# A two-layer streaming-encoder trunk in fp32 pairs: a new order of the attention steps, half of the convolution's taps moved and read from PSUM, and inverse roots by logarithm and exponential

## What is computed

```python
def swiglu(x, w_gate, w_up, w_down):          # 1024 -> 2816 -> 1024
    return (silu(x @ w_gate) * (x @ w_up)) @ w_down

def even_mixer(h, ...):                        # h = rmsnorm(x)
    u, g, q, k, v, f_logit = split(h @ w_in)   # 512 columns each, f_logit 8
    a = u * sigmoid(g)
    a = causal_depthwise_conv(a, conv_w) + conv_b      # 31 taps
    a = silu(rmsnorm(a, conv_norm))            # norm over 512 channels
    q, k = rmsnorm(q, q_norm), rmsnorm(k, k_norm)      # per head, 64 wide
    o = forgetting_attention(q, k, v, log_sigmoid(f_logit + b_f))
    return concatenate([a, o]) @ w_out
# forgetting_attention: logits = q k^T / 8 + cum_f[q] - cum_f[k], causal, softmax, @ v; 8 heads
```

## Time and profile before

| | |
|---|---|
| median of three runs | 1962.81 us |
| profiled execution | 1965.04 us, its span 1963.2 us |
| TensorE matmul busy | 1889.5 us (96%), 8333 instructions |
| VectorE busy | 915.5 us (47%) |
| ScalarE busy | 621.6 us (32%) |
| GpSimd busy | 330.2 us (17%) |
| mean DMA | 89 GB/s |

### The profile page before, as it was taken

The page is one execution under the profiler, slowest core; times in us unless marked ns, Lnnn a source line. Parts: engine busy times, 40 slices in busy tenths (PEclk is TensorE's granted clock), DMA queues, the critical chain, the costliest instruction groups (busy, mean ns, idle before and its releaser), DMA issues.

```text
span 1963.2 us, 22410 instructions
## 1 busy us (share of the span) xinstructions
PE 1889.5 (96%) x8333; PEld 1540.9 (78%) x8333; DVE 915.5 (47%) x1016; ACT 621.6 (32%) x803; POOL 330.2 (17%) x276
## 2 busy tenths in 40 slices
PE   7999999998876899999999999999999999999999
PEld 5888888875555688888888888888888888888887
DVE  6443433379875564343334443433365454343321
ACT  4333332225433443333223333332222333333221
POOL 3111101115444211111101111110113021111000
PEclk9999999999877899999999999999999999999999
DMA  5333333221100143333332333343233333333431
GB/s 142 99 98 96 102 111 100 75 79 54 32 1 6 56 121 96 96 96 108 103 99 75 96 96 96 96 118 99 72 97 96 97 97 96 96 96 100 118 105 42
DMA packets 341356, 174.86 MB, mean 89 GB/s; under 512 B 6256, under 2 KB 340284, under 8 KB 341308
## 3 DMA queue, kind: packets, MB, share of 16 engines
q1 hardware_dynamic: 337052, 172.12, 30.3%
q10 hardware_dynamic: 4256, 2.11, 0.4%
HBM read 172.10 MB, written 2.10 MB: 89 GB/s over the span
## 4 chain that ended last, share of the span: by engine, by line
PE 88%; DVE 7%; ACT 2%; issue 2%; POOL 1%; DMA 0%; SPq 0%; ACTq 0%; POOLq 0%; DVEq 0%
PE bank L1188 29%; PE bank L1189 29%; PE bank L1190 29%; DVE conv L901 3%; DVE w_lo L871 1%; DVE pt_lo L1094 1%; ACT w_hi L587 0%; DMA x_rows<-in_x 0%; DVE h_rough L1032 0%; PE bank L1417 0%; POOL probs_a L547 0%; POOL conv L559 0%; PE bank L1244 0%; DVE neg_max L1087 0%; ACT probs_a L737 0%
## 5 line engine op out<-in xcount | busy, mean ns | idle before, releaser
L871 DVE TENSOR_TENSOR w_lo<-raw,w_hi 128x1024 fp32r<-128x1024 f32 (+2 forms) x308 | 403.0, 1309 | 718.6 <-ACT w_hi L587 718.2
L1188 PE MATMUL bank<-xg_hi,w_hi 128*128 128x512 f32 x1728 | 678.3, 393 | 8.1 <-DVE w_lo L871 4.8
L1189 PE MATMUL bank<-xg_lo,w_hi 128*128 128x512 f32 x1728 | 674.0, 390 | 0.0
L1190 PE MATMUL bank<-xg_hi,w_lo 128*128 128x512 f32 x1728 | 673.8, 390 | 0.0
L587 ACT ACTIVATE w_hi<-raw 128x1024 fp32r<-128x1024 f32 (+2 forms) x308 | 340.3, 1105 | 793.0 <-PE bank L1190 792.9
L1188 PEld LDWEIGHTS bank<-xg_hi,w_hi 128*128 128x128 f32 x1728 | 325.4, 188 | 86.3 <-issue 10.8
L1189 PEld LDWEIGHTS bank<-xg_lo,w_hi 128*128 128x128 f32 x1728 | 325.5, 188 | 68.1 <-issue 1.2
L1190 PEld LDWEIGHTS bank<-xg_hi,w_lo 128*128 128x128 f32 x1728 | 325.3, 188 | 67.8
L1188 PE MATMUL bank<-h_hi,w_hi 128*128 128x512 f32 x704 | 274.5, 390 | 0.0
L1190 PE MATMUL bank<-h_hi,w_lo 128*128 128x512 f32 x704 | 274.0, 389 | 0.0
L1189 PE MATMUL bank<-h_lo,w_hi 128*128 128x512 f32 x704 | 273.9, 389 | 0.0
(11 more groups left out here) (184 smaller groups left out, 1171.3 us busy)
## 6 DMA issues: line engine op xcount, KB each, us to landing
raw<-in_ffn_w_gate SPq DMA_DIRECT2D x88, 512.0 KB, 3.8
raw<-in_ffn_w_up SPq DMA_DIRECT2D x88, 512.0 KB, 3.8
raw<-in_ffn_w_down SPq DMA_DIRECT2D x64, 704.0 KB, 4.5
raw<-in_od_w_in SPq DMA_DIRECT2D x24, 512.0 KB, 3.7
raw<-in_ev_w_in SPq DMA_DIRECT2D x20, 512.0 KB, 3.8
raw<-in_ev_w_out SPq DMA_DIRECT2D x16, 256.0 KB, 2.7
raw<-in_od_w_out SPq DMA_DIRECT2D x8, 512.0 KB, 3.7
x_rows<-in_x SPq DMA_DIRECT2D x4, 512.0 KB, 7.4
```

The source lines that it names most:

```text
L871: dve.tensor_tensor(w_lo[:, u % 2, 0:n], raw[:, u % 4, 0:n], raws(w_hi[:, u % 2, 0:n]), ALU.subtract)\
L1188: pe.matmul(dst, a[0], b[0], start=start, stop=False)
L1189: pe.matmul(dst, a[0], b[1], start=False, stop=False)
L1190: return pe.matmul(dst, a[1], b[0], start=False, stop=stop)
```

## The change

1. Taps. VectorE keeps two tiles (0 and 2), ScalarE with GpSimd gets two (1 and 3). VectorE's source tile now lies in PSUM bank 7: tile 0 is written there directly, tile 2 is copied there by ScalarE when tile 0 is done. Only the last 10 VectorE taps, one a step in attention, read it from SBUF. The forget logits move to bank 5. VectorE's taps are put behind every unit of A_GATE (at most 4), and ScalarE's start in A_GATE (13), then 29 in qk, 12 in v, and 2 in each of the first four steps of attention.
2. Head norms. `head_sum` runs two units late instead of one, with four buffers for squares. The fans of the last three tiles move into attention's steps 0 to 2. The split of v starts tile by tile (`v_done`).
3. Attention. On each engine the work of a step has a new order: the inverse of the last step's sums first, then the maxima, the output's split, the transposed probabilities' split (one step later than before), and the taps. ScalarE does the split ahead of the exponentials. `weigh` is one step later. 22 steps in all. GpSimd scales the probabilities one step later in its program.
4. Convolution's norm. The sum over partitions moves from step 14 to 16, behind the last scores; its silu and split move into the first units of the out phase.
5. Out phase. The attention half comes first for all eight output tiles, and the first three quarters of its first two units are issued in steps 18 and 19.
6. Inverse roots. ScalarE computes Ln and then Exp with factor -0.5; the reciprocals of the norms are gone, the Newton step stays.

```diff
-    DVE_TILES, ACT_TILES = list(range(CB - 1)), [CB - 1]
-    TAPS_A, TAPS_QK = [7, 7, 8, 8], [2, 4, 4, 3, 4, 0, 4, 4]
-    TAPS_T = 3
-    ACT_TAPS_QK, ACT_TAPS_V = [0, 3, 4, 4, 4, 4, 4, 4], 4
+    DVE_TILES, ACT_TILES = [0, 2], [1, 3]
+    TAPS_A, TAPS_QK = [0, 4, 3, 4, 4, 4, 4, 4], [2, 2, 4, 2, 4, 1, 4, 4]
+    TAPS_T = 1
+    ACT_TAPS_A, ACT_TAPS_QK, ACT_TAPS_V, ACT_TAPS_T = [3, 3, 4, 3], [2, 3, 4, 4, 4, 4, 4, 4], [4, 4, 4], 2
-    V_FANS = [(1, 1), (1, 3), (2, 1), (2, 3), (3, 0), (3, 2)]
+    V_FANS = [(1, 2), (2, 1), (3, 1)]
-    TURN_LAG = 2
-    PV_LAG = 3
-    OUT_LAG = PV_LAG + 1
-    STEPS = PAIRS + OUT_LAG
-    NEXT_SPLIT = (12, 16)
+    INV_AT, TURN_AT, PT_AT, PV_AT, OUT_AT = 1, 2, 3, 5, 8
+    STEPS = TB * (AB - 1) + OUT_AT + 2
+    NEXT_SPLIT = (12, 14)
+    A_SQ, A_SUM = [4, 6, 8, 14], PAIRS
+    MERGE_AT = (STEPS - 4, STEPS - 3)
+    SILU_AT = [(0, 2), (0, 3), (1, 0), (1, 1)]
...
             def norm_root(ready, n, mean, out_log, out_rough, done):
+                logs[0] += 1
                 act.wait_ge(ready, n)
-                act.activation(out_root, mean, ACT.Sqrt).then_inc(done, 1)
+                act.activation(out_log, mean, ACT.Ln).then_inc(log_ready, 1)
+                act.wait_ge(log_ready, logs[0])
+                act.activation(out_rough, out_log, ACT.Exp, scale=-0.5).then_inc(done, 1)
...
+                        if i == 1:
+                            act.wait_ge(conv_done, 1)
+                            act.activation(bank[7][:, :], a_in[:, DVE_TILES[1], :], ACT.Copy).then_inc(conv_moved, 1)
...
                 elif ph.kind == "v":
...
                     qk_high(0)
                     split_hi(ph, 0, 2)
+                    conv_taps(ACT_TAPS_V[0])
                     qk_high(1)
+                    conv_taps(ACT_TAPS_V[1])
                     qk_high(2)
+                    split_hi(ph, 0, 3)
+                    conv_taps(ACT_TAPS_V[2])
                     qk_high(3)
-                    split_hi(ph, 0, 3)
-                    conv_taps(ACT_TAPS_V)
-                    for n in range(AB, QK - 1):
-                        qk_high(n)
+                    qk_high(4)
...
             def conv_taps(n, late=False):
+                    src = a_in[:, b, :] if late else bank[7][:, :]
-                        op = dve.scalar_tensor_tensor(conv[:, b, shift:S], a_in[:, b, 0:S - shift], wk,
+                        op = dve.scalar_tensor_tensor(conv[:, b, shift:S], src[:, 0:S - shift], wk,
                                                       conv[:, b, shift:S], ALU.mult, ALU.add)
...
+                            split_lo(ph, g, 3)
                             dve.wait_ge(root_ready, ph.norm + 1)
-                            link(dve.reciprocal(rough[:, :], root[:, :]))
-                            split_lo(ph, g, 3)
                             invert(mean_sq[:, :], rough[:, :], corr[:, :], rstd[:, :]).then_inc(rstd_ready, 1)
...
                 for t in range(STEPS):
+                    if 0 <= t - INV_AT < PAIRS:
+                        cols = slice(2 * (t - INV_AT), 2 * (t - INV_AT) + 2)
+                        dve.wait_ge(exp_done, 2 * (t - INV_AT) + 2)
+                        dve.reciprocal(row_inv[:, cols], row_sum[:, cols]).then_inc(inv_ready, 1)
                     if t < PAIRS:
                         for i in (2 * t, 2 * t + 1):
...
-                    if 0 <= t - TURN_LAG < PAIRS:
...
+                    if 0 <= t - PT_AT < PAIRS:
...
-                    if t < PAIRS:
-                        dve.wait_ge(exp_done, 2 * t + 2)
-                        dve.reciprocal(row_inv[:, 2 * t:2 * t + 2], row_sum[:, 2 * t:2 * t + 2]).then_inc(inv_ready, 1)
...
+                    if QK - 3 + t < QK:
+                        qk_low(QK - 3 + t)
-                    conv_taps(TAPS_T)
+                    conv_taps(TAPS_T, late=True)
...
                 for t in range(STEPS):
                     if t < PAIRS:
                         scores(t)
+                    if t == A_SUM:
+                        pe.wait_ge(exp_done, 2 * t)
+                        pe.wait_ge(a_added, CB - 1)
+                        pe.matmul(bank[3][:, :], ones[:, :], sq_sum[:, :], start=True, stop=True).then_inc(a_sum, 1)
+                    if QK - 3 + t < QK:
+                        fan(QK - 3 + t)
+                    for par in range(2):
+                        chunk = every(t, PV_AT + par, 2, CHUNKS)
+                        if chunk is not None:
+                            weigh(chunk, par)
+                    if 0 <= t - TURN_AT < PAIRS:
+                        turn(t - TURN_AT)
+                    if t in MERGE_AT:
+                        n = MERGE_AT.index(t)
+                        pe.wait_ge(wlo_ready, A_OUT.unit0 + n + 1)
+                        merge_part(A_OUT, 0, n, list(range(CB - 1)))
...
-                        if i:
-                            head_sum(i - 1)
+                        if i >= 2:
+                            head_sum(i - 2)
```

306 lines of the change are left out of this document (160 added, 146 removed).

## The result

The changed kernel takes 1919.3 us, the median of 4 runs (1918.7 to 1921.0); the kernel before takes 1964.1 in the same series (1962.7 to 1965.5). The ratio is 0.9773, with a 95% interval of 0.9756 to 0.9790: 44.8 us less, against 45 forecast. The sum is right, but most of its terms are not, and they are what the rest is about.

The account below looks back on a forecast made before the run. Outside the first mixer TensorE was the bound; gains lay between 382 and 700 us, in waits behind VectorE's queue. Gains 12 + 9 + 20 + 4 = 45 us from 1962.8 gave 1918 us, range 1903 to 1945.

Parts of the forecast that it names:

- the first scores: Start of attention: as a sign of being right, the first scores come some 21 us earlier.
- A_GATE and qk, 12 forecast: First mixer stages: 114 us become 102, with PSUM taps at 0.70 us and 2.6 us of waits.
- The two-input rule: VectorE taps: only two SBUF inputs contend with GpSimd reading SBUF; by it A_GATE and qk gain 1 us more.
- v, 9 forecast: v stage: 48 us become 38.5 to 39, TensorE waiting 7 us for the last unit's w_lo.
- ScalarE waiting for GpSimd's adds in qk or v: qk and v: a sign that the forecast is wrong, ScalarE waiting for GpSimd's conv adds.
- that rival: qk and v: GpSimd becomes the bound, adds at 1.9 us, gain 30, 1933 us; chance 0.09.
- Attention, 20 forecast: First to last scores: 91.2 us fall by 20; four steps at 5.0, eleven at 4.6, the 11.1 us wait gone.
- The loop that I found last: Attention step: scores, maxima, output split, both splits of the step before, then the second tile's turn; 4.3 us.
- The steps don't get shorter: Attention: handshakes and low clock set the pace, only the stall goes, gain 10 there, 1928 us; chance 0.17.
- Tail, 4 forecast: Last scores to next phase: 65.0 us become 60.5 to 61, with waits listed for splits, Ln and Exp, weights and clock.
- The other norms, 0 forecast: Six norms of other phases: Ln, load and Exp end 0.9 us ahead of w_hi, so they gain and cost nothing.
- The rule by which the load between them would fall away: Ln and Exp share one table set, needing one load; by it tail and v would each be 1.3 us shorter.

Follow-up runs that it names:

- tile2_sbuf: Changed kernel with VectorE's second conv tile of taps read from SBUF instead of its PSUM copy: 1931.1 us.
- v_quiet: Changed kernel with v's weight splits ahead of ScalarE's taps, four taps moved into attention, the logits' splits and scan moved: 1911.6 us.
- sum_at_14: Changed kernel with the convolution norm's sum over partitions put back in front of step 14's scores: 1930.4 us.
- old_split: Changed kernel with the splits inside an attention step back in their old order, weigh steps as changed: 1927.0 us.
- merge_late: Changed kernel without the early start of the output projection, all its products behind the attention: 1918.5 us.
- before_no_late_taps: Kernel before the change with 36 of its 38 VectorE taps in attention left out (convolution incomplete): 1939.2 us.
- more_taps: Changed kernel with two extra VectorE taps from SBUF in each of 16 attention steps, results thrown away: 1931.1 us.
- both: Changed kernel with old_split's order and v_quiet's v part, its eight ScalarE taps placed four and four: 1911.9 us.
- both_pv4: The kernel both with the weigh steps one step earlier, as in the kernel before: 1909.9 us.
- v_split_first: Changed kernel with w_lo of v's last unit ahead of k's low part and the logits' splits, k's high part before ScalarE's third four taps: 1916.9 us.

## Why the prediction was right, and where it was not

The sum, 45 us less, was met (44.8 by the medians, 46.0 by the profiled executions) because errors cancel: v was 8.6 and A_GATE with qk 2.6 too high, the attention 6.2 and the tail 3.9 too low, and 2.1 came from a start that varies by itself. So close a sum is luck; what held is that all of the gain lies in the mixer and most of it in the attention. Of the signs that I had named, the first scores came 12 us earlier and not 21, mainly because v gave nothing.

*A_GATE and qk, 12 forecast, 9.4 measured (10.9 by the four kernels with 103.1).* The price of a tap from PSUM was right: 0.70 taken, 0.733 measured, and tile2_sbuf shows that it is the operand's place and not GpSimd's leisure. The two-input rule of the Trainium skill ("SBUF — State Buffer", "Who interferes with whom") agrees with the taps of tile2_sbuf in one stretch: 0.717 us with one input in PSUM, 1.273 with both in SBUF. But that price is not the whole gain: undoing it for tile 2 took back 3.4 us in this stage (4.9 against the 103.1). The kernel before waited 5.3 us here for the squares of the head sums and the changed one not at all; I hadn't priced that, and no run separates the later head sums from the shorter queue of VectorE. What I left out is that the other instructions of VectorE pay for GpSimd's adds: the scan of the logits stands in front of a `w_lo`, which itself takes 1.98 us, and TensorE waits 2.06 at 463.81. v_quiet, with the scan behind it, has 101.6 us, my 102.

*v, 9 forecast, 0.4 measured.* The mechanism was the right one, TensorE waiting for `w_lo` of v's last unit; the chain was mis-sized. I had 31 us from qk's end to that `w_lo`; it ended at 522.29, 37.9 after 484.40. Newton's instructions are 1.64 and 1.62 us and not 0.7, two of the logits' splits 1.5 and not 0.7, both under GpSimd's adds; and I counted ScalarE's products as lying in between, while four of them (2.9 us) stood in front of `k_hi`. The rest, 9.8 us for 7.5 behind the wait, is a wait of 0.9 for `v_lo` and the slow clock (0.80 from 522.3 to 532.1 us). I had named ScalarE waiting for GpSimd's adds in qk or v as a sign that GpSimd is the bound: it came, in five waits of 2.9 us in all, 0.38 of them in the queue at whose end TensorE waited 11.5. GpSimd wasn't the bound (an add took 1.35 us on average, and that rival needed 1.9); what I hadn't asked is what stands behind the products in ScalarE's queue, and behind `k_lo` in VectorE's.

*Attention, 20 forecast, 26.2 measured.* The loop that I found last is the one that TensorE's nine waits for `pt_lo` show, and by rows it gave 4.3 us; steps 8 to 11 took 4.13. The step of the sum that failed is the 0.3 that I added for the clock: it was 1.00 from step 6 on, 0.93 over the eleven steps. The eleven steps took 47.0 us, 4.27 each for 4.6, and the first four 4.5 for 5.0: 5.6 of the 6.2. In the first four the reason was wrong: I had GpSimd busy for 20 us there, and it was busy for 12.7 of 18.0, while the clock was 0.72 and TensorE waited 2.7 us for the probabilities and 1.8 for `pt_lo`. "The steps don't get shorter" fell with 4.13 us. The moved sum was worth 8 to 11 us (sum_at_14), and the earlier trace rows had 11.1.

*Tail, 4 forecast, 7.9 measured.* I listed 7.5 us of waits and slow clock; 2.7 came, 1.5 for `cat_lo`, 0.8 for `w_lo` and 0.4 for `pt_lo`, at full clock. By old_split, the new order of `cat_hi` and `cat_lo` is what keeps the tail short, which I hadn't seen as a gain at all; the early merges, which I had taken for one, bring nothing (merge_late).

*The other norms, 0 forecast, 0.0 measured.* This is right as described: a load lies between Ln and Exp, and ScalarE's `w_hi` still waits for TensorE. ffn2's norm:

```profile
662.94 0.63 ACT L623 ACTIVATE log_mean<-mean_sq 128x512 f32<-128x512 f32 x1 [0.59 <-DVE mean_sq L974]
663.59 1.28 ACT L625 ACT_TABLE_LOAD   x1
664.88 0.63 ACT L625 ACTIVATE rough<-log_mean 128x512 f32<-128x512 f32 x1
666.33 1.06 ACT L605 ACTIVATE w_hi<-raw 128x1024 fp32r<-128x1024 f32 x1 [0.82 <-PE bank L1222]
```

The cover is 0.82 us, 0.9 in the forecast. The rule by which the load between them would fall away (the Trainium skill, "ScalarE: Activation LUTs", "Table sets: the hidden batching unit") isn't met by this trace: 1.28 us each time.

*The parts, undone one by one,* are in the mixer 8.9 (tile 2 in PSUM), 8.1 (the sum), 6.9 (the order), 0.9 (Ln and Exp) and nothing (the merges), 24.8 of 43.8 us, if they add. A likely part of the rest is the 26 late taps fewer (12 for 38): at 0.71 each, by before_no_late_taps, they are 18, at 0.30, by more_taps, 8. Another is the later head sums, with 7.3 us of waits gone. No run undid either alone, nor the first stages' other taps, so 19 us of the gain are explained by inference only.

## What to carry to other kernels

Price an instruction by what runs beside it, not by its mean elsewhere: the same subtraction took 1.2 or 2.0 us, depending on another engine's adds. In a queue in program order, ask of every filler what stands behind it and who paces it: in v, 3 us of conv products and 4.4 us of splits that nobody needed yet stood in front of the one split that TensorE waited 11.5 us for. And where a loop's waits are small and many, a new order tends to move them to another name: look for the slots in which an engine already waits (in old_split VectorE, 1.0 to 1.25 us between each `neg_max` and `pt_lo`) and put the filler there.

## What the runs showed of the hardware that I had not expected

The clock behind a short wait isn't settled by the code. both and both_pv4 have the same instructions up to step 3 of the attention and the same wait of 2.0 us ahead of the first scores. TensorE's stretches from there on, of the one and of the other:

```profile
517.61:532.84 15.23, 15.23 (x52) 8.34 (x52) 9.14 (x17) 8.10 (x19) 11.77 (x17) 0.52 0.00 1
```

```profile
517.27:526.42 9.15, 8.76 (x50) 5.05 (x50) 5.87 (x11) 4.61 (x11) 6.55 (x13) 1.00 0.00 1
```

The granted clock is 0.52, nearly all at the lower level of 1.2 GHz, in the one and 1.00 in the other, 15.2 against 9.2 us for the first three steps with their fans and the first turn. The fast one then waited 4.7 us for `pt_lo`, and in the end the first four steps took 16.6 us for 18.2: here the clock moved the wait more than the time. v_quiet and v_split_first, with 5.8 and 3.8 us of waiting there, gave back 2.9 and 2.8 us of what they had gained in v. In these kernels, a gain ahead of the first steps was worth less than its size.
